# One inference step of a hybrid decoder: first weight chunk of the projection loaded and split by halves, first products placed before the third tile's turns

## The reference

```python
D_MODEL, SEQ, DEC_BATCH, DEC_SEQ = 1024, 1024, 8, 8
def rmsnorm(x, w):
    xf = x.astype(jnp.float32)
    y = xf * lax.rsqrt(jnp.mean(xf * xf, axis=-1, keepdims=True) + EPS)
    return (y * w.astype(jnp.float32)).astype(x.dtype)
def decoder_layer(x, kv_buf, mlstm_state, p):
    xn = rmsnorm(x, p["attn_norm_w"])
    proj = xn @ p["w_in"]          # (1024 + 64 tokens) x 1024 @ 1024 x columns, float32
    ...
```

## Time and profile before

| what | value |
|---|---|
| median of 3 runs | 1499.63 us (1498.01 to 1501.52) |
| the profiled execution | 1500.26 us |
| its span, first to last instruction | 1498.5 us |
| mean granted TensorE clock | 0.975 |
| PE busy | 1410.8 us (94%) |
| DVE busy | 1003.0 us (67%) |
| ACT busy | 726.7 us (48%) |

### The profile page before, as it was taken

One profiled execution on the slowest core, in us unless ns is written; L12 is line 12 of the kernel. 1 busy time (PEld: TensorE's weight loads), 2 busy tenths in 40 slices (PEclk: granted clock), 3 DMA queues, 4 the chain that ended last, 5 costly groups with the idle time before them and its releaser, 6 DMA issues.

```text
span 1498.5 us, 21458 instructions
## 1 busy us (share of the span) xinstructions
PE 1410.8 (94%) x8013; PEld 1193.8 (80%) x8013; DVE 1003.0 (67%) x1341; ACT 726.7 (48%) x861; POOL 212.8 (14%) x243
## 2 busy tenths in 40 slices
PE   5999999999999999999999879999999999999990
PEld 5999999998999998899788656777777777777760
DVE  4522321167666667776566678888888888888875
ACT  6421121144444445423212247777777777777760
POOL 2600000021111111000200041241111111111014
PEclk9999999999999999999999889999999999999995
DMA  6346423243333324658621389999999999999938
GB/s 199 119 130 212 140 79 70 75 136 114 125 121 115 105 73 118 195 170 261 266 91 42 109 334 379 354 384 402 392 393 388 391 392 391 398 395 394 377 129 316
DMA packets 135895, 347.40 MB, mean 232 GB/s; under 512 B 13768, under 2 KB 92044, under 8 KB 110160
## 3 DMA queue, kind: packets, MB, share of 16 engines
q1 hardware_dynamic: 125672, 312.32, 57.8%
q0 software_dynamic: 6048, 21.50, 4.7%
q10 hardware_dynamic: 4120, 12.85, 2.2%
HBM read 292.34 MB, written 55.28 MB: 232 GB/s over the span
## 4 chain that ended last, share of the span: by engine, by line
PE 45%; DVE 3%; DMA 1%; ACT 1%; issue 1%; POOL 1%; POOLq 0%; ACTq 0%; DVEq 0%
PE xt_ey L2550 4%; PE xt_ey L2551 4%; PE xt_ey L2552 4%; PE y_h_up L2529 4%; PE y_h_up L2528 4%; PE y_h_up L2530 4%; PE logits_gate L2528 2%; PE logits_gate L2530 2%; PE logits_gate L2529 2%; PE ranks_gate L2528 2%; PE ranks_gate L2530 2%; PE ranks_gate L2529 2%; PE y_x L2517 2%; DVE e_w_lo L2409 1%; PE y_x L2084 1%; PE y_h_up L2084 1%
## 5 line engine op out<-in xcount | busy, mean ns | idle before, releaser
L2409 DVE TENSOR_TENSOR e_w_lo<-mixed,e_w_hi 128x2048 fp32r<-128x2048 f32 x64 | 145.8, 2296 | 2.0 <-ACT e_w_hi L2342 2.0
L2409 DVE TENSOR_TENSOR e_w_lo<-w_out,e_w_hi 128x2048 fp32r<-128x2048 f32 x64 | 143.6, 2283 | 2.9 <-ACT e_w_hi L2342 2.9
L987 PE MATMUL gate_banks<-f_hi,wg_hi 128*128 128x364 f32 (+1 forms) x376 | 126.8, 337 | 0.9 <-DVE wg_lo L855 0.4
L2342 ACT CAST e_w_hi<-mixed 128x2048 fp32r<-128x2048 f32 x62 | 117.0, 1912 | 15.3 <-ACT e_y_rows L2363 8.9
L988 PE MATMUL gate_banks<-f_lo,wg_hi 128*128 128x364 f32 (+1 forms) x376 | 123.5, 328 | 0.0
L989 PE MATMUL gate_banks<-f_hi,wg_lo 128*128 128x364 f32 (+1 forms) x376 | 123.4, 328 | 0.0
L2342 ACT CAST e_w_hi<-w_out 128x2048 fp32r<-128x2048 f32 x64 | 121.8, 1904 | 0.6 <-ACT e_y_rows L2363 0.6
L2550 PE MATMUL xt_ey<-e_w_hi,e_hT_hi 128*96 128x512 f32 x256 | 103.5, 404 | 5.1 <-DVE e_w_lo L2409 3.9
L2271 POOL CAST idx<-token_of_slot 96x1 uint32 (+1 forms) x30 | 50.3, 1677 | 401.9 <-PE y_x L2517 368.5
L2551 PE MATMUL xt_ey<-e_w_lo,e_hT_hi 128*96 128x512 f32 x256 | 102.0, 398 | 0.0
L2528 PE MATMUL y_h_up<-e_w_hi,e_x_hi 128*96 128x512 f32 x256 | 100.7, 394 | 0.7 <-DVE e_w_lo L2409 0.7
(11 more groups left out here) (624 smaller groups left out, 3598.0 us busy)
## 6 DMA issues: line engine op xcount, KB each, us to landing
w_out<-in_w_down_e SPq DMA_DIRECT2D x64, 1024.0 KB, 7.9
mixed<-in_w_gate_e SPq DMA_DIRECT2D x32, 1024.0 KB, 6.8
mixed<-in_w_up_e SPq DMA_DIRECT2D x32, 1024.0 KB, 8.3
w_gate<-in_w_gate_e SPq DMA_DIRECT2D x32, 1024.0 KB, 6.9
w_up<-in_w_up_e SPq DMA_DIRECT2D x32, 1024.0 KB
expert_rows<-e_y_rows ACTq DMA_DIRECT2D x32, 384.0 KB, 7.2
proj<-mixed SPq DMA_DIRECT2D x8, 1408.0 KB, 5.6
w_ring<-in_w_in SPq DMA_DIRECT2D x7, 1408.0 KB, 10.6
```

The lines of the kernel that those rows point to most:

```text
L987: pe.matmul(bank, wg_hi[j][:, k, :], hi, start=(k == 0), stop=False)
L2342: act.copy(hi(i, step, j), raw(i, u, j)).then_inc(hi_ready[i], 1)
L2409: dve.tensor_tensor(lo(i, u, j), raw(i, u, j), hi(i, step, j).bitcast(F32), ALU.subtract).then_inc(lo_ready[i], 1)
```

## The change

The first weight chunk comes by two DMAs, k 0 to 3 and k 4 to 7, each with a semaphore of its own, and ACT and DVE split it in the same two halves. On ACT the first half is cast before `feat_hi(0)`, the second behind it. On DVE the order of the beginning is written anew. On PE the turns of tile 0 and 1 come first; then each iteration does a product and behind it the turns of the tile two further on. So product t - 1 (and no longer t - 2) stands behind the turns of tile t. The first product waits for the low weights twice, once for each half. Counts of the semaphores are moved by one for the buffer of the even chunks.

```diff
@@ block.sync
-                        load(0)
+                        for i, ks in enumerate(FIRST_HALVES):
+                            sp.dma_start(w_ring[0][:, ks, 0:width[0]], w_view[:, ks, columns(0, width[0])]).then_inc(w_loaded[0] if i else first_half_loaded, 16)
@@ block.scalar
+                def first_split_hi(i):
+                    ks = FIRST_HALVES[i]
+                    act.wait_ge(w_loaded[0] if i else first_half_loaded, 16)
+                    act.copy(w_hi[0][:, ks, 0:width[0]], w_ring[0][:, ks, 0:width[0]]).then_inc(w_hi_ready[0], 1)
...
                 scale(1)
+                first_split_hi(0)
                 feat_hi(0, P)
-                split_hi(0)
+                first_split_hi(1)
                 for t in range(2, NT + 1):
@@ block.vector
-                for t in range(NT + 1):
+                turned(0, P)
+                first_split_lo(0)
+                feat_lo(0, P)
+                first_split_lo(1)
+                turned(1, P)
+                feat_lo(1, P)
+                for t in range(2, NT + 1):
                     turned(t, tile_rows(t))
-                    if t:
+                    if t > 2:
                         feat_lo(t - 1, P)
-                    if t == 1:
-                        split_lo(0)
@@ block.tensor
                     for k in range(KD):
+                        if first and k % (KD // 2) == 0:
+                            pe.wait_ge(w_lo_ready[0], k // (KD // 2) + 1)
...
-                    if t >= 2:
-                        if t == 2:
-                            pe.wait_ge(w_lo_ready[0], 1)
-                        pe.wait_ge(f_lo_ready, t - 1)
-                        product(0, 0, t - 2, width[0])
+
+                turn_x(0)
+                turn_x(1)
+                for t in range(NT - 1):
+                    pe.wait_ge(f_lo_ready, t + 1)
+                    product(0, 0, t, width[0], t == 0)
+                    turn_x(t + 2)
```

More of the change, by code:

```diff
@@ L156, in project @@
         w_loaded = [sem(f"w_loaded{v}") for v in range(2)]
+        first_half_loaded = sem("first_half_loaded")
         full = [sem(f"pj_full{b}") for b in range(6)]
@@ L171, in project @@
         seqs = lambda ap: ap[:, TP:T].rearrange("h (c t) -> h c t", t=ST)
+        FIRST_HALVES = (slice(0, KD // 2), slice(KD // 2, KD))
         def columns(n, w):
@@ L245, in _ @@
                 for n in range(NCH - 2):
-                    sp.wait_ge(w_lo_ready[n % 2], n // 2 + 1)
+                    sp.wait_ge(w_lo_ready[n % 2], n // 2 + 2 - n % 2)
                     load(n + 2)
@@ L255, in _ @@
                 sp.dma_start(a["m_sample"][0].rearrange("b h -> h b"), m_last[:, 8:16]).then_inc(rows_stored, 16)
-                sp.wait_ge(w_lo_ready[0], NCH // 2)
+                sp.wait_ge(w_lo_ready[0], NCH // 2 + 1)
                 for j in range(2):
@@ L406, in split_lo, with first_split_lo @@
                     w = width[n != 0]
-                    dve.wait_ge(w_hi_ready[v], cc + 1)
+                    dve.wait_ge(w_hi_ready[v], cc + 2 - v)
                     dve.tensor_tensor(w_lo[v][:, :, 0:w], w_ring[v][:, :, 0:w], w_hi[v][:, :, 0:w].bitcast(F32), ALU.subtract).then_inc(w_lo_ready[v], 1)
+                def first_split_lo(i):
+                    ks = FIRST_HALVES[i]
+                    dve.wait_ge(w_hi_ready[0], i + 1)
+                    dve.tensor_tensor(w_lo[0][:, ks, 0:width[0]], w_ring[0][:, ks, 0:width[0]], w_hi[0][:, ks, 0:width[0]].bitcast(F32), ALU.subtract).then_inc(w_lo_ready[0], 1)
                 rows = Own(dve, row_step)
@@ L505, in _, with product @@
                 pe.wait_ge(ms_ready, 6)
-                def product(cc, v, t, w=CW):
+                def product(cc, v, t, w=CW, first=False):
                     b, r = 3 * v + t % 3, tile_rows(t)
@@ L525, in product, with turn_x @@
                     ins.then_inc(full[b], 1)
-                for t in range(NT + 1):
+                def turn_x(t):
                     r = tile_rows(t)
@@ L553, in _ @@
                     for v in range(2):
-                        pe.wait_ge(w_lo_ready[v], cc + 1)
+                        pe.wait_ge(w_lo_ready[v], cc + 2 - v)
                         for t in range(NT + 1):
@@ L557, in _ @@
                 for v in range(2):
-                    pe.wait_ge(w_lo_ready[v], NCH // 2)
+                    pe.wait_ge(w_lo_ready[v], NCH // 2 + 1 - v)
                     for t in range(NT + 1):
```

## The result

The changed kernel takes 1518.46 us in the median of 4 runs, the kernel before 1500.58 beside it. Ratio of the runs: 1.0109, 95% interval 1.0095 to 1.0124, so 16.4 us slower (14.3 to 18.6); the two medians lie 17.9 apart. The forecast was 15.0 slower, 1514.6 us, with a range from 1508 to 1520.5. In the sets of runs behind this one, three executions in a slow state (1601 to 4544 us) are in the medians that are given but not in the ratios, and every "us faster" or "us slower" goes by the ratio. Its profiled execution took 1515.59, span 1513.8, 15.3 more than the span before; it is the shortest of the four.

The account below looks back on a forecast made before the run. PE, busy 94% of the span, was taken to bound the kernel: -6.0 lead + 8.0 + 6.4 + 2.0 gaps - 0.3 wait = +10.1, plus 4.9 clock = +15.0 us, so 1514.6 us; range 1508 to 1520.5.

Parts of the forecast that it names:

- Halves, product 0, turns of tile 2: Ramp over chunk 0: halved load and splits let product 0 start at 13.8 and the turns of tile 2 at 19.1.
- rival 3: Early product not early: first half lands late or product 0 at half clock; lead 3.2, total 1517.4 us; chance 0.12.
- Lead: PE in the ramp: turns 0 to 3 and products 0 and 1 done 6.0 us sooner than at 30.73.
- Gaps: PE waits for DVE before products 2 to 7: 8.0 us (tiles 3, 4, 6), 6.4 (5, 7), 2.0 (8).
- Clock: PE falls to half clock behind three of the six gaps, 1.6 us each, 4.9 us in all.
- the dropped 0.3: PE's wait of 0.30 us for `scale(8)` goes, since ACT has more time.
- Rival 4: Not slower: DVE's chain ends within 1.05 us of the turns' end; with no gaps 1493.3 us; chance 0.02.

Follow-up runs that it names:

- the first experiment: Changed kernel with DVE's low features of a tile right behind its `turned`, in front of the next tile's turns, emptying earlier: 1500.26 us, ratio 0.9988 to the kernel before.
- the filled kernel: Changed kernel plus ten matmuls that nobody reads behind the turns of tiles 3 to 8: 1510.89 us, ratio 1.0062 to the kernel before.
- square of tile 8 sooner: Changed kernel with low features right behind `turned(t)`, plus ACT's square of tile 8 ahead of chunk 1's high weights: 1498.13 us, ratio 0.9970 to the kernel before.
- best version: Changed kernel with low features behind `turned(t)`, chunk 1's low weights in halves, ACT squaring a tile ahead, scaling before high features: 1495.33 us, ratio 0.9967 to kernel before.

## Why the prediction was right

Direction, size and the range hold. By its own steps, in the two profiles of the changed kernel:

- *Halves, product 0, turns of tile 2.* Forecast 13.8 and 19.1; measured 14.31 and 19.32 in the first, where all starts 0.46 later since the first tile's DMA landed so much later, and 13.83 and 19.63 in the second. The first half was there in time: ACT's cast follows the scaling without a pause in both. In the first, product 0 ran at full clock and ended 0.80 before the turns could start, held by `scale(2)` as said. In the second its matmuls start 0.30 apart up to 17.60, the distance of the half clock, and product 0 itself set the turns: `scale(2)` was done at 18.80, 0.8 before them. The condition named for rival 3 thus occurs, at a smaller price.
- *Lead.* Forecast 6.0. Turns 0 to 3 and products 0 and 1 were done at 25.0 (24.21 + 0.79) against 30.73: 5.7. In the second profile it is 5.5.
- *Gaps.* Forecast 2.66 between the turns' end and the product for tiles 3, 4 and 6, 3.2 for 5 and 7, 2.0 for 8. Measured in the same way: 27.65 - 25.00 = 2.65, 2.64, 2.64; 3.32 and 3.32; 2.12. Sum 16.7 against 16.4. (The bracketed idle times are some 0.25 less, since the last transposes run on.) DVE had 1.64 us to spare between chunk 1's low weights and `turned(8)`, not the half microsecond of the forecast, which changes nothing. The place was shown by the first experiment, which removes them, and by the one with PE's order alone, which makes them; the 0.65 surplus by the emptying moved.
- *Clock.* Forecast three falls, 1.6 each. Measured two and three, 1.55 each: 3.1 and 4.6 against the 4.9 taken. With lead, gaps and the dropped 0.3 this gives the ramp of both profiles, 13.8 and 15.6 longer than before. By the distance to the filled kernel the clock would cost 5.8 to 7.6, which the profiles do not show. If that is right, this term is mis-sized by one to three us, enough for the difference between 15.0 and the measured 16.4.
- *Luck.* Three falls was the middle between none and six, and that the runs come so near to it is partly luck. Its grounds were three idle stretches, each seen in one execution. In the later traces two of them go the other way as well (see the last section), so they could bear the range and not the number. The page "TensorE: Matmul & The Clock Gate" of the Trainium skill, section "A second HAM failure mode: psum-queue depth-cycling", tells of a kernel in which short idle times between groups of matmuls make the clock swing. The two traces agree, but for only a part of the gaps: two and three of six.
- *Rivals.* None of the profiled executions was without a fall, none had six. Rival 4, the lead kept, needs another order on DVE; with one, and another on ACT, the ramp kept 5.9 us (61.77 to 55.89) and the time 5.0 of the 6.3 reckoned for that rival.

What I had not seen is POOL. The prediction gives ACT's cast and DVE's low weights as the reason for the 7.42 us of idleness before. The last link was another: POOL's addition for tile 2, 2.11 us beside these low weights, kept ACT waiting for 1.77 of them. At 0.19 the turns of tile 2 could have started some 1.8 us sooner (an estimate: `scale(2)` at 16.6, behind the high features of tile 1, in place of 18.39). In the changed kernel this addition takes 1.00 beside half of the low weights and holds nothing up, so the forecast of 19.1 did not suffer. For tile 8 it is a limit that only a faster ramp meets, and it stands behind the miss of the first experiment.

## What to carry to other kernels

When a consumer's program is advanced by one step, look on the producer's engine for what stands in front of the operand: an operand made "behind the next tile's input" is free as long as the consumer is two tiles behind and a stall per tile once it is one behind. Move both programs, or neither: PE's order alone cost 22.8 us and the halves alone changed nothing that could be measured. PE's and DVE's order with the halves gained 1.8, and 5.0 only when ACT's order was moved too. (DVE's order alone was not run.) When one wait is gone, look at every engine in the chain to the next one, small instructions included. A gap of 2 to 3 us on TensorE should be priced with the half clock that may follow, and that price varies from one execution to the next.

## What the runs showed of the hardware

- Work that nobody reads made the kernel about 7 us faster: ten matmuls in each of six gaps kept the granted clock at 1.00 from 20 to 72, where the same waits without them brought it to 0.50 two or three times.
- Whether the clock falls behind a short gap changes from one execution to the next, with the same gap at the same place. That of 1.78 us brought no fall in the kernel before. It stands in all eleven traces, 1.78 or 1.79 long, and brought one in three of them (square of tile 8 sooner, gaps filled, best version). That of 2.49 at 721.80 stands in all eleven too, 2.49 or 2.50 long, and brought one in eight of them; with low features in front, with the gaps filled and in the best version PEclk stays at 1.00. The length of a gap does not decide it. The gap of 1.79 in the best version, then with low features in front:

```profile
205.79 0.43 PE L553 MATMUL pj<-w_hi,f_hi 128*128 128x352 f32 x1 [1.79 <-ACTq L201]
```

```profile
207.00:210.00 3.00, 3.00 (x13) 3.00 (x12) 0.00 (x0) 0.00 (x0) 0.00 (x0) 0.50 0.00 0
```

```profile
211.68 0.43 PE L541 MATMUL pj<-w_hi,f_hi 128*128 128x352 f32 x1 [1.79 <-ACTq L201]
```

```profile
213.00:216.00 3.00, 3.00 (x21) 3.00 (x20) 0.17 (x1) 0.00 (x0) 0.00 (x0) 1.00 0.00 0
```

- A GpSimd addition of 64x1 took 2.30 us beside a DVE subtraction of 128x2816 from SBUF, and 0.18 us away from one; it ended 0.05 after DVE's instruction. The addition for tile 2 stands beside DVE's low weights of chunk 0 in all eleven traces: it took 2.11 to 2.19 where these are made whole and 1.00 where they are made in halves, and ended 0.04 to 0.05 behind them each time. Beside `turned`, which reads PSUM, such an addition took 0.19. The Trainium skill, page "GPSIMD Engine Reference", section "1. Specifications", says that GpSimd shares its SBUF interfaces with VectorE, with contention for VectorE instructions of two SBUF inputs; the traces agree with that. No run took DVE's subtraction away with everything else in place, so the cause rests on the ends that coincide and on the placements.
